# Another order of the Q, K and V projections in a one-core hybrid transformer block

## What is computed

```
mod   = silu(c) @ w_mod + b_mod                  # six groups of 1024 numbers; the same for the context
p     = modulate(rms_norm(x), sh1, sc1) @ w_in   # and the same product for the context tokens
hy, q, k, v, nq, nk, nv = split(p)
q, k  = rope(rms_norm(q)), rope(rms_norm(k))     # the context's k: the norm alone; nq, nk: neither
gqa   = attend(q, [k_ctx, k], [v_ctx, v])        # 8 heads of queries, 2 of keys
na    = neighbourhood_attention(nq, nk, nv) with a bias table, and the context's keys   # 4 heads
hyo   = x2 * (fft_long_conv(v_h * x1) + v_h * x1 * skip)     # v_h, x1, x2 = split(short_conv(hy))
x     = x + gt1 * ([hyo, gqa, na] @ w_out)
x     = x + gt2 * swiglu(modulate(rms_norm(x), sh2, sc2))
out   = rms_norm(x) * g_final
```

## Time and profile before

| | |
|---|---|
| median of 3 runs | 1445.65 us (1443.83 to 1446.08) |
| profiled execution | 1450.32 us, span 1448.5 us |
| mean granted TensorE clock | 0.974 of full speed |
| busy share of the span | PE 94%, DVE 69%, ACT 47%, POOL 17% |

### The profile page before, as it was taken

The page is one execution under the profiler, slowest core; times in us unless marked ns, Lnnn a source line. Parts: engine busy times, 40 slices in busy tenths (PEclk is TensorE's granted clock), DMA queues, the critical chain, the costliest instruction groups (busy, mean ns, idle before and its releaser), DMA issues. The chain is left out here.

```text
span 1448.5 us, 24255 instructions
## 1 busy us (share of the span) xinstructions
PE 1356.5 (94%) x8353; PEld 745.1 (51%) x8353; DVE 1004.7 (69%) x1612; ACT 685.7 (47%) x1307; POOL 241.2 (17%) x165
## 2 busy tenths in 40 slices
PE   5989978789968899999999999999999999999997
PEld 0274545345446677777754554444444444444443
DVE  2686588757568889999943579766666666676477
ACT  0451212343257788888842255444444444521235
POOL 0000011114024094000000022332323231000001
PEclk9899999999979999999999999999999999999999
DMA  6815311043422030030001122222222222598853
GB/s 231 343 34 199 116 59 58 30 131 120 171 59 48 1 118 14 15 87 0 1 16 43 44 73 81 80 80 80 80 80 80 80 80 80 206 330 319 314 196 139
DMA packets 119610, 156.23 MB, mean 108 GB/s; under 512 B 18707, under 2 KB 80381, under 8 KB 118269
## 3 DMA queue, kind: packets, MB, share of 16 engines
q1 hardware_dynamic: 113419, 152.32, 31.4%
q10 hardware_dynamic: 6130, 3.11, 0.7%
HBM read 132.98 MB, written 22.42 MB: 107 GB/s over the span
## 5 line engine op out<-in xcount | busy, mean ns | idle before, releaser
L958 PE MATMUL PS<-arena 128*128 128x512 f16 (+6 forms) x7048 | 1230.2, 333 | 32.2 <-DMA arena<-in_hy_f_wout 9.2
L958 PEld LDWEIGHTS PS<-arena 128*128 128x128 f16 (+3 forms) x7048 | 613.5, 103 | 589.9 <-issue 54.2
L2303 DVE SCALAR_TENSOR_TENSOR arena<-arena 128x512 f16<-128x512 f32 x148 | 120.2, 818 | 76.2 <-ACT arena L1716 76.2
L1716 ACT ACTIVATE arena<-arena 128x512 f16<-128x512 f32 x140 | 87.6, 629 | 130.4 <-PE PS L958 130.4
L2247 DVE SCALAR_TENSOR_TENSOR arena<-PS,arena 128x512 f16<-128x512 f32 (+2 forms) x256 | 139.9, 598 | 6.8 <-ACT arena L1659 4.8
L1659 ACT ACTIVATE arena<-PS 128x512 f16<-128x512 f32 (+2 forms) x256 | 118.7, 531 | 52.8 <-PE PS L1254 52.7
L1254 PE MATMUL PS<-arena 128*128 128x128 f32 x864 | 116.5, 281 | 8.1 <-ACT arena L1649 7.9
L1649 ACT ACTIVATE arena<-PS,arena 128x1280 f32<-128x1280 f32 (+1 forms) x96 | 118.0, 1230 | 1.1
L1254 PEld LDWEIGHTS PS<-arena 128*128 128x128 f32 x864 | 94.3, 142 | 46.9 <-ACT arena L1649 46.1
L2239 DVE TENSOR_REDUCE arena<-PS 128x1 f32<-128x1280 f32 x64 | 95.4, 1491 | 23.0 <-PE PS L958 23.0
L1828 ACT ACTIVATE arena<-arena 128x512 f16<-128x512 f32 x77 | 48.1, 629 | 128.8 <-DVE arena L2452 74.1
(11 more groups left out here) (179 smaller groups left out, 1054.4 us busy)
## 6 DMA issues: line engine op xcount, KB each, us to landing
arena<-in_w_ffn_out SPq DMA_DIRECT2D x121, 256.0 KB, 4.9
arena<-in_w_mod SPq DMA_DIRECT2D x24, 1024.0 KB, 5.3
arena<-in_w_ffn_in SPq DMA_DIRECT2D x88, 256.0 KB, 3.0
arena<-in_w_in SPq DMA_DIRECT2D x9, 1024.0 KB, 5.0
left_operands<-arena SPq DMA_DIRECT2D x33, 256.0 KB, 2.2
arena<-left_operands SPq DMA_DIRECT2D x3, 2816.0 KB, 14.3
arena<-in_x SPq DMA_DIRECT2D x2, 2048.0 KB, 17.4
arena<-cst_fwd SPq DMA_DIRECT2D x4, 1024.0 KB, 11.7
```

The lines of the kernel that those rows point to most:

```text
L958: return pe.matmul(out, lhsT, rhs, start=start, stop=stop, skip_group_check=True)
L1716: act.activation(aS[n % RING][:, 0], weight_block(p, b), ACT.Copy, scale=WS).then_inc(blk_hi, 1)
L2303: dve.scalar_tensor_tensor(dst[:, 1], src, WS, dst[:, 0], ALU.mult, ALU.subtract).then_inc(blk_lo, 1)
```

## The change

The groups come in the order (2, 0, 1). With that:

- The convolution's VectorE pieces lie between the slots of the first group, now NA's K and V. Buffers are moved for it: `r0`, `r1` share X's place, so `residues(1)` waits for the first fold; `multiply` uses one scratch buffer instead of two, one step after the other; `output` leaves its low half to `output_lo`, two parts at a time. The inverse products come ahead of units 6 and 7.
- Eight late parts instead of four lie in the short convolution, two behind each of its first four tiles, with the second column sums ahead of the transposes of v. Their chunks move forward in `CHUNKS`. Both Q/K/V splits lie behind tile 4, the gain tables behind tile 5.
- The eight other late parts lie behind the slots of unit 17 to unit 24. Column sums 2 go behind unit 22, column sums 3 behind unit 26; each set has its own accumulator.
- The last group (1) has its own PSUM banks (6 and 7; turned in 5 and 2) and work buffers. The loops of three rounds are written out.
- GpSimd masks head 0's table behind the power of the last group's first unit and adds its five kinds behind the next five; head 1's mask follows the seventh.
- TensorE's first scores come ahead of the last projection; the last turns and the last late sum lie between the first attention steps, on ScalarE and VectorE too.

The order of the loads, the buffers and the banks:

```
-CHUNKS = (["mod"] * 8 + ["ff", "ff", "hy", "hy", "late", "hy", "late", "late", "late", "qkv", "qkv", "fwd", "fwd",
-                         "inv", "inv"] + ["qkv"] * 4 + ["late"] * 12 + ["wo"] * 4)
+CHUNKS = (["mod"] * 8 + ["ff", "ff", "hy", "hy", "late", "late", "hy"] + ["late"] * 6 + ["qkv", "qkv", "fwd", "fwd",
+                                                                                     "inv", "inv"]
+          + ["qkv"] * 4 + ["late"] * 8 + ["wo"] * 4)
...
-        macc = [f32(Z, GW)] + [f32(30, GW)] * 3
+        macc = [f32(o, GW) for o in (Z, Z + 4, 29, 33)]
-        r0, r1 = f32(Z + 83, 2, HYW), f32(Z + 85, 2, HYW)
+        r0, r1 = f32(44, 2, HYW), f32(46, 2, HYW)
...
-        GROUPS = (0, 1, 2)
+        GROUPS = (2, 0, 1)
...
+        def bank_of(u):
+            return u % 2 + 6 * (UNITS[u][0] == 1)
+        def turned_bank(u):
+            if UNITS[u][0] != 1:
+                return 2 + u % 2
+            return 7 if u == NU - 1 else (5, 2)[u % 2]
+        def work(u):
+            return u % 2 + 2 * (UNITS[u][0] == 1)
```

GpSimd, behind the power of each unit:

```
+                if g == 1 and t == 0:
+                    pool.wait_ge(pr_mm, GROUP0[1])
+                    column_mask(0)
+                    own.wait()
+                if g == 1 and 1 <= t < 6:
+                    bias_of(0, t - 1)
+                if g == 1 and t == 6:
+                    column_mask(1)
```

TensorE:

```
-            for ct in range(5):
+            for ct in range(4):
                 hyena(ct)
             pe.wait_ge(spec_rdy, 2)
             late_columns(0, 6)
+            hyena(4)
+            late_columns(1, 7)
...
             forward(0)
             pe.wait_ge(hy_rdy, 6)
-            project(0, 0, 0, 0, False)
+            project(0)
+            project(1)
             pe.wait_ge(spec_rdy, 3)
             forward(1)
...
+            for u in range(2, NU):
+                if u == 6:
                     pe.wait_ge(spec_rdy, 4)
+                    inverse(0)
+                if u == 7:
+                    inverse(1)
+                if u in (GROUP0[0], GROUP0[1]):
+                    pe.wait_ge(split_lo, 7 if u == GROUP0[0] else 9)
+                if u == NU - 1:
+                    break
+                project(u)
+                turn_qk(u - 2)
+                if u == GROUP0[1] + 4:
+                    late_columns(2, 4)
+            late_columns(3, 4)
...
+            scores(Unit(0))
+            project(NU - 1)
+            turn_qk(NU - 3)
+            pe.wait_ge(late_rdy, 4)
+            scores(Unit(1))
+            turn_qk(NU - 2)
+            pe.wait_ge(pr_tc, NU - 2)
+            turn_p(Unit(0))
+            turn_qk(NU - 1)
+            pe.wait_ge(pr_tc, NU - 1)
+            attend(Unit(1))
             pe.wait_ge(pr_tc, NU)
-            scores(Unit(0))
-            late_columns(3, 7)
-            for v in range(3):
-                attend(Unit(v))
+            attend(Unit(2))
```

ScalarE:

```
-                if ct in (3, 4):
-                    hi_of(chunk_index("qkv", ct - 3), spl(ct - 1, 4, 512))
+                if ct == 4:
+                    for b in range(2):
+                        hi_of(chunk_index("qkv", b), spl(2 + b, 4, 512))
...
                 if kt:
-                    act.wait_ge(spec_rdy, 2 + kt)
+                    act.wait_ge(G_rdy, kt)
...
                 if g == 0:
-                    ins = act.copy(qT[:, :, tok(t + m)], ps)
+                    if t == 0:
+
+                        act.wait_ge(y_rdy, 4)
+                    ins = act.copy(qT[:, :, tok(t)], ps)
...
+            slot(NU - 1)
             exponentials(Unit(0))
+            hi_parts(NU - 1)
+            turned(NU - 2)
+            copy_p(Unit(0))
+            exponentials(Unit(1))
+            turned(NU - 1)
```

VectorE:

```
             residue_sums(0)
+            slot(0)
             multiply(0)
-            slot(0)
             slot(1)
             fold(0)
+            slot(2)
             residue_sums(1)
-            slot(2)
             slot(3)
             multiply(1)
+            slot(4)
             fold(1)
-            for u in range(4, NT):
+            for u in range(5, GROUP0[0]):
                 slot(u)
...
+            for u in range(GROUP0[0], NU - 1):
                 slot(u)
+                if u in (GROUP0[0] + 2, GROUP0[0] + 3):
+                    i = u - GROUP0[0] - 2
+                    lo_of(chunk_index("qkv", 4 + i), spl(2 + i, 4, 512))
+                if GROUP0[1] - 1 <= u < GROUP0[1] + 7:
                     late(n)
                     n = n + 1
+                if u == GROUP0[1] + 5:
+                    late_sum(2)
...
             maximum(Unit(0))
+            slot(NU - 1)
+            late_sum(3)
+            dve.wait_ge(late_rdy, 4)
+            modulation_gain(af, 32, V_GFFN, 1)
+            maximum(Unit(1))
+            lo_parts(NU - 1)
+            low_p(Unit(0))
+            inverse_sum(Unit(0))
```

More of the change, by code:

```diff
@@ L605, in arrived, with stacks @@
             eng.wait_ge(raw_in[chunk_slot(c)], more * 16 + 16 * chunk_arrivals(c))
-        def stacks(g, t, par):
-            out = []
+        def stacks(u):
+            (g, t), par, out = UNITS[u], work(u), []
             n_k = {1: HKV, 2: HN, 0: 0}[g]
@@ L712, in _ @@
                 if h == 1:
-                    for n in range(4, 16):
+                    for n in range(8, 16):
                         g, kp = n // 4 + 2, n % 4
@@ L875, in _ @@
                     .then_inc(pr_rs, 1)
[L877 to L880, removed]
+                if g == 1 and t == 0:
[6 more added lines that the diff above has]
+                    column_mask(1)
+            for h in range(1, HN):
+                if h == 1:
+                    pool.wait_ge(pr_mm, NU)
+                    pool.wait_ge(pr_tm, NU)
+                else:
+                    column_mask(h)
+                    pool.wait_ge(bias_add, NT * (h - 1))
                 own.wait()
[L883 to L886, removed]
                 for kind in range(5):
[L888 to L891, removed]
+                    bias_of(h, kind)
             for n in range(4):
@@ L1607, in slot @@
                 if u >= 2:
-                    turned(u - 2, it)
+                    turned(u - 2)
             residues(0)
             slot(0)
+            slot(1)
             residues(1)
-            for u in range(1, NT):
+            for u in range(2, GROUP0[0]):
                 slot(u)
@@ L2046, in _ @@
                     lo_of(chunk_index("hy", 2), spl(0, KD, 256))
[L2047 to L2048 removed]
                 if ct < 4:
[L2050 removed]
+                    late(2 * ct)
+                    late(2 * ct + 1)
                 if ct == 4:
+                    for b in range(2):
+                        lo_of(chunk_index("qkv", b), spl(2 + b, 4, 512))
                     late_sum(0)
[L2053 removed]
+                    late_sum(1)
+                if ct == 5:
                     dve.wait_ge(gn_in, 32)
@@ L2197, in _ @@
                 if u in (6, 7):
-                    output(u - 6)
-            u0 = GROUP0[1]
-            for b in range(2):
-                slot(u0 + b)
-                output(2 + b)
-            for b in range(2):
-                lo_of(chunk_index("qkv", 4 + b), spl(2 + b, 4, 512))
-            with dve.Fori(0, 3) as it:
-                own.enter(it, 8)
-                for b in range(2):
-                    slot(u0 + 2 + b, it)
-                own.leave(3)
-            slot(u0 + 8)
-            slot(u0 + 9)
@@ L2264, in _ @@
             maximum(Unit(0))
-            for v in range(NNA + 1):
+            slot(NU - 1)
[6 more added lines that the diff above has]
+            inverse_sum(Unit(0))
+            for v in range(1, NNA + 1):
                 attend(Unit(v))
```

280 lines of the change are left out of this document (122 added, 158 removed).

## The result

The changed kernel takes 1409.83 us (median of four, 1406.72 to 1410.57), the kernel before 1445.87 beside it: 36.0 us less, a ratio of 0.9748 with a 95% interval of 0.9729 to 0.9766. The forecast was 1414, the range 1402 to 1427. The profiled execution of the changed kernel took 1410.57, its span 1408.8; the one of before was 4.4 above its own median.

A forecast was written before the change was run, and what follows sets the result against it. TensorE was taken to wait 33.9 us for VectorE's low halves of q and k, with clock falls behind waits. First scores 33.5 us earlier, less 2.1 given back, made 31.4 off the median 1445.65: 1414, range 1402 to 1427.

The forecast's parts named there:

- Short convolution: Modulation parts moved there: 3.5 us together plus one clock fall of 2.3; forward product 0 starts 5.8 later, at 179.5.
- First group: NA's K and V beside the convolution: no TensorE wait over 0.6 us; first Q projection ends at 268.0.
- Second group: Q: VectorE sets the pace, eight slots of 5.86 us from 268.8 plus 4.5 of weight splits, to 320.2; clock stands.
- Third group: K/V and NA's Q: modulation parts 20.8, slots 21.1, GpSimd's disturbance 8.8, an addition 0.2; from 320.2 to 371.1.
- the rival of the full block: Third group: every GpSimd addition and mask stops VectorE for its whole length, 15.0 instead of 8.8; 1420; chance 0.10.
- The skewed bias: Its table, written at about 271, is in by 327, mask due at about 325: nothing to 2 us, taken as nothing.
- The end: First scores at 376.6, 33.5 earlier; second unit's probabilities turned 13.7 later instead of 11.65, so 2.1 given back.
- The sum: 33.5 - 2.1 = 31.4 us of gain, subtracted from the median 1445.65: 1414.3, so 1414.
- The forecast's own case: The likeliest case, 1414, chance 0.61; own bounds 1405 (no disturbance) and 1420 (full).
- more gain: GpSimd's additions fall into VectorE's waits, the clock never falls, up to 4 at the tail: 1399 to 1403; chance 0.12.
- the clock's rival: Nine small waits in the second and third group bring the clock down; five falls give 11 us: 1425; chance 0.10.
- the last two rivals: Convolution's parts still late for the units, 1432, chance 0.05; first mask waits for the skewed table, 1452, chance 0.02.

The follow-up runs named there:

- the copies first: Changed kernel with ScalarE's four copies of the turned v ahead of the two high parts of NA's weights; 1406.33 us.
- The extra work: Changed kernel plus six 512-wide VectorE multiplications in each of the first eight slots of NA's K and V; 1436.51 us.
- the old order of the pieces: Changed kernel, groups in the new order, but the convolution's VectorE pieces in the order they had before; 1416.20 us.
- the low halves moved: Changed kernel with VectorE's two low parts of the K/V weights cut in halves and laid into the middle of four slots; 1407.17 us.
- the third edit: Changed kernel with the last sum of the late columns ahead of the first maximum on VectorE; alone 1407.50 us.
- the kernel with its end apart: Changed kernel with all projections and turns first again, then the first scores, on each engine; 1409.40 us.
- the gates later: Changed kernel with SyncE waiting for the third unit's output ahead of the gates' DMA; 1409.56 us.
- the spreading: Kernel before, Q group still first, with the convolution's pieces laid one by one between slots 0 to 4; 1449.78 us.

## Why the prediction was right

*Short convolution.* 5.8 predicted in four terms; the last products end at 179.20 against 179.5. The wait is 2.64 (0.84 + 1.9 = 2.74), and the clock fell, as taken. The run with the copies first shows that wait and fall are this order's price: its last products end at 173.96, 5.2 earlier by the profiles. The median keeps 3.1 of that.

*First group.* Predicted: no wait over 0.6 us, end of the first Q projection 268.0. Measured: none at all, 267.49. The extra work shows that the reason was the right one, and the old order of the pieces that the light group alone would leave some 6 us lying.

*Second group.* Slot 5.86, predicted 5.86; begins 268.12 against 268.8, ends 319.43 (the projection behind it is on TensorE by then) against 320.2. The waits are 0.49 to 1.60, as said. "I let the clock stand" was wrong in one place: behind the 1.60 at 299.74 a projection took 7.04 instead of 5.35. It cost nothing there, as VectorE set the pace. With the low halves moved, these waits went, and TensorE set the pace at 5.63 from turn to turn.

*Third group.* This step was mis-sized. Predicted from 320.2 to 371.1, 50.9 us; measured from 319.43 to unit 25's slot at 365.26, 45.8. A slot without a part of the modulation takes 2.67 (365.26 to 367.93), not the 3.02 of the earlier trace rows, where gaps lay between the operations; over seven, 2.5. A part takes 2.51 rather than 2.6, and the first of each set 1.98, so eight take 19.0 and not 20.8. And GpSimd's disturbance is 7.8 and not 8.8: its operations are 1.25 and 2.62 us here, not the 1.55 and 3.60 of the earlier trace rows, and VectorE loses 7.8 of these 11.5, 0.68, where I had 0.59 of the longer times. Together 5.3, for a difference of 5.1. One sign that I gave did not come: no part of the modulation was slower beside GpSimd's additions, its two operations took 2.60 as they do alone. What met GpSimd's operations was the rotation's L2195, which comes right behind the power, and the slots were 5.9 instead of 6.5.

*The rule on the shared port.* It was the rival of the full block, at 15.0. The Trainium skill, "SBUF — State Buffer", section "Who interferes with whom", is right in its mechanism: L2195, with two inputs in SBUF, ends with GpSimd's operation each time. But the block is what is left of that operation when VectorE arrives, so its whole length was an upper bound that this program never meets. The operation ahead of L2195 has one input in PSUM and kept its 0.29 us.

*The skewed bias.* Costed at nothing, rightly: the write goes out at 267.94, and the first mask follows the power at once, without a wait for its table.

*The end.* Predicted: first scores at 376.6, second unit turned 13.7 later, at 390.3. Measured: 368.88 and 380.38, 11.5 apart. Of the 9.9 us between the two ends, 0.8 lie at the start of the third group and 5.1 in it. Another 1.9 lie between unit 25's slot and the scores: the wait of "some 4 us" for unit 24 is 2.65, and its turn and the last column sums took 2.4 and not 4.3, since the clock fell only behind them. The last 2.2 are the overlap's own: I took 13.7 as if the last projection stood whole in the path; it lies mostly beside ScalarE's and VectorE's work. But I did not see what the third edit showed: the last sum of the modulation, behind the last slot on VectorE, keeps the second scores waiting 2.12 us, and its gates' transfer is still under way when the heads' loop begins. By the profiles these two come to about what the overlap won; the kernel with its end apart took the same time, but medians can't tell 2 us, so that this is the reason is likely and not shown.

*The sum.* I had 31.4 up to the second unit's turn; by the profiles it came 41.4 earlier (421.74 to 380.38). At the fifth unit's turn 40.3 are left, behind the pause, at the ends of the spans 39.7, and in the medians 36.0, because the profiled execution of before was 4.4 above its median and the one of after 0.7. I noted that gap and still took a gain read from the slow profile off the median. So the gain was 10 us too small, most of it in the third group and the end, and this step happened to take back nearly 4 of them: that 1414 is only some 4 from the measured time is in part luck. Taken off the profile's own 1450.32, my 31.4 would have given 1418.9, still inside the range, but 8 to 9 off.

*Rivals.* The forecast's own case came in. Of "more gain" only the shorter tail came: its condition did not, as GpSimd's operations cost VectorE 7.8 us and the clock fell three times (at 165, 300 and 368). Of the clock's rival one of the falls came, the one behind the 1.60 us wait at 299.74, and it lay off the path. Of the last two rivals no sign is there: from 166.82 to 289.80 TensorE waits for no piece of the convolution, and the first mask waits for no table.

## What to carry to other kernels

When one engine feeds two streams, put the stream that needs little of it beside the burst of the other; spreading the burst beside a stream that needs much of it only moved the wait to the next consumer (3.9 us slower in the kernel before), beside the light stream it was worth 6. A wait ahead of one-column products cost twice here, by its length and by the clock behind it: 2.65 us of wait went with 1.6 to 4.3 us of slower products. With the end apart the same wait of 2.66 stood ahead of the last projection, which took 2.78 us at full clock, and sixteen one-column products behind it 1.90. So look at what stands behind a wait: it can be worth more than its length, and a helper's operation that makes it, like one mask of 2.62 us, is worth moving. Take a gain off the time of the same execution that it was read from.

## What was not expected of the hardware

*A pause at the loop's entry while the gates' writes have not landed.* SyncE's program reads the gates back once its writes of them have landed, some 11 us after it issued them (388.17 in the kernel after). The packets themselves had moved long before. Kernel after, 377 to 380 us, then 380 to 385:

```profile
DMA packets 2080, 0.01 MB, mean 3 GB/s; under 512 B 2080, under 2 KB 2080, under 8 KB 2080
```

```profile
DMA packets 0, 0.00 MB, mean 0 GB/s; under 512 B 0, under 2 KB 0, under 8 KB 0
```

The pause, from 385.9 to 388.4, begins some 7 us behind the last of them. In the five profiles where the heads' loop was entered 1.2 us or more before the writes had landed (the kernel after twice, the extra work, the copies first, the gates later), ScalarE, and VectorE in four of them, paused 1.3 to 2.4 us with a release that the trace calls "remote". In seven others they landed before the loop or 0.4 us behind its entry, and none shows more than 0.3. In the kernel before, with and without the spreading, they had landed before the loop too (426.17 and 429.29, the loop from 428.30 and 431.24): the change moved the loop ahead of the landing. So the pause goes with the landing, and moves with it in the kernel with the gates later; what exactly is held up, and by what, stays open, and nothing was tried that tells it.

*The same wait, different falls.* Behind the same wait of 2.65 or 2.66 us for unit 24's low half, the same 46 products took 6.95 or 6.96 us in four profiles and 8.31 to 9.64 in five others; in the two where the wait was 0.56 or less, 5.30. Such falls may be some of the 3 to 5 us by which executions of one kernel differ; no run shows that. The spread of 6.4 us behind the mark was not looked into.
